# Decoder layer on one core: first modulation by slices of 256 features, squares of four units summed at once, second-norm modulation moved into the output projection

## The reference

```python
mod = silu(c) @ w_ada + b_ada                      # c: one row; w_ada: 1024 x 6144
shift1, scale1, gate1, shift2, scale2, gate2 = split(mod, 6)
h = rms_norm(x, norm1_g) * (1 + scale1) + shift1
q, k, v, qi, ki, wi, u_pool, g_attn, g_pool = split_cols(h @ w_in)
q, k = rms_norm per head of 64                     # 8 heads
attn = top-128 sparse attention(q, k, v, indexer qi, ki, wi)
y_attn = attn @ w_attn_br
y_pool = multiscale_pool(u_pool, w_grp, pool_scale) @ w_pool_br
merged = sigmoid(g_attn) * y_attn + sigmoid(g_pool) * y_pool
x = x + gate1 * (merged @ w_out)
h2 = rms_norm(x, norm2_g) * (1 + scale2) + shift2
x = x + gate2 * conv_ffn(h2, w_up, conv_w, conv_b, w_down)   # d_ff 2816, taps 3
```

## Time and profile before

| | |
|---|---|
| median of 3 runs (lowest to highest) | 754.72 us (754.32 to 757.94) |
| profiled execution: its own time, its span | 759.15 us, 757.2 us |
| PE busy | 739.7 us, 98% of the span |
| DVE, ACT, POOL busy | 379.0, 306.6, 312.3 us |
| DMA | 92.75 MB, mean 122 GB/s |
| mean granted clock of TensorE | 0.986 of 2.4 GHz |

### The profile page before, as it was taken

One profiled execution on the slowest core, in us unless ns is written; L12 is line 12 of the kernel. 1 busy time (PEld: TensorE's weight loads), 2 busy tenths in 40 slices (PEclk: granted clock), 3 DMA queues, 4 the chain that ended last, 5 costly groups with the idle time before them and its releaser, 6 DMA issues.

```text
span 757.2 us, 9497 instructions
## 1 busy us (share of the span) xinstructions
PE 739.7 (98%) x3568; PEld 597.2 (79%) x3568; DVE 379.0 (50%) x693; ACT 306.6 (40%) x501; POOL 312.3 (41%) x165
## 2 busy tenths in 40 slices
PE   4989999999999999999999999999999999999997
PEld 3467788888777777887899888888788888888886
DVE  2588699972446551774685435464443433004002
ACT  4224513256756763334455343434334343212120
POOL 1125338562623332547423444444444444443431
PEclk9969989999999999999999999999999999999999
DMA  8995511221113113644338344323323321233301
GB/s 327 381 338 204 187 55 57 71 97 56 57 57 112 57 56 107 262 159 128 97 95 267 112 111 112 91 76 112 101 68 110 111 99 68 84 112 112 137 2 56
DMA packets 83995, 92.75 MB, mean 122 GB/s; under 512 B 2035, under 2 KB 66287, under 8 KB 83951
## 3 DMA queue, kind: packets, MB, share of 16 engines
q1 hardware_dynamic: 82719, 87.43, 35.6%
q10 hardware_dynamic: 1232, 4.72, 1.7%
HBM read 90.05 MB, written 2.10 MB: 122 GB/s over the span
## 4 chain that ended last, share of the span: by engine, by line
PE 96%; DVE 1%; DMA 1%; ACT 1%; SPq 0%; issue 0%; DVEq 0%; ACTq 0%
PE bank L1471 42%; PE bank L1491 21%; PE bank L1480 21%; PE bank L1547 2%; PE bank L1741 1%; PE bank L1719 1%; PE bank L1707 1%; PE bank L1513 1%; PE bank L1625 1%; DMA xtok<-in_x_dram 1%; PE bank L1565 1%; PE bank L1614 1%; ACT junk L747 1%; PE bank L1518 1%; PE bank L1775 1%; PE bank L1532 0%
## 5 line engine op out<-in xcount | busy, mean ns | idle before, releaser
L650 POOL TENSOR_TENSOR wsplit<-stage,wsplit 128x1024 fp32r<-128x1024 f32 (+1 forms) x120 | 275.0, 2295 | 395.2 <-ACT wsplit L732 391.7
L1471 PE MATMUL bank<-hT,wsplit 128*128 128x512 f32 (+1 forms) x1264 | 295.3, 386 | 0.0
L1471 PEld LDWEIGHTS bank<-hT,wsplit 128*128 128x128 f32 x1264 | 231.8, 190 | 46.5 <-issue 0.9
L732 ACT ACTIVATE wsplit<-stage 128x1024 fp32r<-128x1024 f32 (+1 forms) x120 | 119.8, 1000 | 280.9 <-PE bank L1480 196.7
L1480 PE MATMUL bank<-hT,wsplit 128*128 128x512 f32 (+1 forms) x632 | 152.8, 384 | 0.0
L1480 PEld LDWEIGHTS bank<-hT,wsplit 128*128 128x128 f32 x632 | 114.7, 188 | 23.5 <-issue 0.8
L1491 PE MATMUL bank<-wsplit,guT 128*128 128x512 f32 x528 | 119.8, 389 | 0.0
L1491 PEld LDWEIGHTS bank<-wsplit,guT 128*128 128x128 f32 x528 | 99.1, 188 | 20.5
L1429 DVE SCALAR_TENSOR_TENSOR yb<-bank,conv,yb 128x511 f32<-128x511 f32 (+1 forms) x44 | 32.9, 749 | 65.1 <-ACT yb L1022 64.3
L1429 DVE SCALAR_TENSOR_TENSOR ya<-bank,conv,ya 128x511 f32<-128x511 f32 (+1 forms) x44 | 33.0, 749 | 59.2 <-ACT ya L1022 58.4
L1364 DVE TENSOR_TENSOR tmp_last<-bank,gate_row 128x512 f32<-128x512 f32 x8 | 5.5, 688 | 101.7 <-PE bank L1491 101.7
(11 more groups left out here) (188 smaller groups left out, 731.8 us busy)
## 6 DMA issues: line engine op xcount, KB each, us to landing
stage<-in_w_up_dram SPq DMA_DIRECT2D x44, 512.0 KB, 5.2
stage<-in_w_in_dram SPq DMA_DIRECT2D x17, 1024.0 KB, 5.3
stage<-in_w_down_dram SPq DMA_DIRECT2D x10, 1024.0 KB, 5.0
ada_early<-in_w_ada_dram SPq DMA_DIRECT2D x8, 1024.0 KB, 10.1
ada<-in_w_ada_dram SPq DMA_DIRECT2D x7, 1024.0 KB, 11.7
ada_mid<-in_w_ada_dram ACTq DMA_DIRECT2D x4, 1024.0 KB, 8.1
stage<-in_w_out_dram SPq DMA_DIRECT2D x4, 1024.0 KB, 6.1
ada_last<-in_w_ada_dram SPq DMA_DIRECT2D x4, 1024.0 KB, 11.1
```

Of the source, the lines that this page charges most:

```text
L650: pool.tensor_tensor(unit_split(n, 1), unit_source(n), unit_split(n, 0).bitcast(F32), ALU.subtract).then_inc(low, 1)
L732: me.did(act.activation(unit_split(n, 0), unit_source(n), ACT.Copy), high)
L1471: pe.matmul(out_bank[:, tokens], hi[:, k, :], rhs[:, part, k, tokens], start=k == 0 and part == 0, stop=False)
```

## The change

1. **Start.** x is normalised token tile by token tile before it is transposed (`xn`; the scaling by the root is on VectorE). shift1 and scale1 are made in four slices of 2 x 256 features: `load_first(q)` brings 128 x 8 x 512 values in two halves, in rows of 1 KB. `first_sums` multiplies them with `cpad` (silu(c), padded to 32 columns), four input blocks at once into four groups of 32 partitions of one bank, two rounds; ScalarE copies, `first_columns` sums over partitions into columns, and VectorE makes two blocks of `hT` from it. All seven first units (qi 0, 1, kw, q 0 to 3) are accumulated side by side in seven banks, input block by input block. Their weights come as items of 2 x 896 columns, one behind each slice, and their low parts are made on VectorE.
2. **Order.** v follows, with the index dots between its blocks, then u, then k. The four squares of q go to TensorE at once (`squares`: `halves`, padded to 32 columns, as weights, 512 tokens, four groups of partitions), are copied and transposed (`squares_turn`); the same for k.
3. **Second norm.** The row additions of shift2 and scale2 (j = 3, 4) are no longer made from `ada_early` beside q. ScalarE's queue loads them through the two `ada_mid` buffers in the output projection, VectorE adds the first set ahead of `gate_vector(0)` and the second behind it, both ahead of the residuals, and TensorE turns them into columns after the first and the second tile of the second half.
4. Window sums get a second pair of buffers; c is loaded from ScalarE's queue; two activation tables are called up early.

The core of the diff:

```diff
-ROW_TURN = {1: 0, 3: 1, 4: 2, 2: 3, 5: 4}
+ROW_TURN = {2: 0, 3: 1, 4: 2, 5: 3}
+FIRST = (("qi", 0), ("qi", 1), ("kw", 0), ("q", 0), ("q", 1), ("q", 2), ("q", 3))
...
+            def load_first(q):
+                for half in range(2):
+                    ks = slice(half * KQ, (half + 1) * KQ)
+                    for j in range(2):
+                        c0 = j * D + 2 * q * P
+                        sp.dma_start(ada_first[q][:, ks, 2 * j * P:2 * (j + 1) * P], ada[:, ks, c0:c0 + 2 * P]
+                                     ).then_inc(ada_in[q][half], 16)
...
             for n, item in enumerate(sch.items):
-                if n == NSTAGE:
-                    for q in range(KD // 2):
-                        load_early(3, q)
...
+                if n < KQ:
+                    load_first(n)
...
 # ScalarE
+            load_mid(4)
+            load_mid(5)
             high_parts(sch.unit["out", 1, NT - 1] + 1)
+            for n in range(6, 12):
+                load_mid(n)
...
 # VectorE
+            for t in range(NT):
+                dve.wait_ge(root_ok, t + 1)
+                me.did(dve.reciprocal(tstat[:, 3, t:t + 1], tstat[:, 2, t:t + 1]))
+                me.settle()
+                me.did(dve.tensor_scalar(xn[:, t, :], xtok[:, t, :], tstat[:, 3, t:t + 1], None, ALU.mult), xn_ok)
...
+            for q in range(KQ):
+                first_vectors(q)
+                for k in (2 * q, 2 * q + 1):
...
+                    me.did(dve.tensor_scalar(full1[:, k % 2, :], xT[:, k, :], gs[:, 0, k:k + 1], mod[:, k:k + 1],
+                                             ALU.mult, ALU.add), n_ok)
+                for k in (2 * q, 2 * q + 1):
+                    first_low(k)
+                    low_parts(k + 1)
...
             merged_low(KD - 1)
+            for q in range(KD // 2):
+                mod_rows(3, q)
             gate_vector(0)
+            for q in range(KD // 2):
+                mod_rows(4, q)
...
 # TensorE
+            def first_sums(q):
...
+                for half in range(2):
+                    pe.wait_ge(ada_in[q][half], 32)
+                    for g in range(KQ):
+                        k = half * KQ + g
+                        mm = pe.matmul(OB[32 * g:32 * (g + 1), :], cpad[:, k, :], ada_first[q][:, k, :],
+                                       start=half == 0, stop=half == 1)
+                mm.then_inc(sums_ok, 1)
...
+            for k in range(KD - 1):
+                first_products(k, h_hi, 0, 0, start=k == 0)
+                if k % 2:
+                    first_columns(k // 2 + 1)
+                first_products(k, h_lo, 1, 0)
+                first_products(k, h_hi, 0, 1).then_inc(used, 1)
+                if k % 2 == 0 and k < KD - 2:
+                    first_sums(k // 2 + 1)
...
+            def squares(part):
+                pe.wait_ge(sq_ok, KA * (part + 1))
...
+                for g in range(KA):
+                    mm = pe.matmul(SUMS[part][0][32 * g:32 * (g + 1), :], halves[:, :], sq[part][g][:, :],
+                                   start=True, stop=True)
+                mm.then_inc(sq_used, 1)
...
+            index_dots(0)
+            await_bank(pe, ("v", 0))
+            value_high(0, 0, 3)
+            index_dots(2)
+            value_high(0, 3, 6)
+            index_dots(4)
...
                 if t == 1:
                     await_drained(pe, ("wo", 0, NT - 1))
                     pe.wait_ge(gate_ok, 2)
+                    pe.wait_ge(mod_ok, 2)
...
+                if t == 0:
+                    pe.wait_ge(gate_ok, 2)
+                    mod_columns(3)
                 if t == 1:
+                    mod_columns(4)
                     x2_turn(0)
```

More of the change, by code:

```diff
@@ L138, in split, with first @@
             self.unit[name] = len(self.units) - 1
+    def first(self):
+        for q in range(KQ):
+            self.items.append(("first", "in", (C_Q, C_QI), 2 * q, 2 * q + 2, 1))
+            self.last_use.append(None)
+            for r in range(2):
+                self.units.append((1, r, KS))
+                self.house()
+                self.item_of.append(q)
+                self.last_use[q] = ("unit", len(self.units))
+        for at, name in enumerate(FIRST):
+            self.opens(name, "dve", FIRST_BANK[at])
+        self.ring = NBANK - 1
     def block_rows(self, w, k0, k1, half, home=None):
@@ L179, in schedule @@
     s = Schedule()
[L180 removed]
+    s.first()
+    for kind, n in (("v", KA), ("u", KA)):
         for m in range(n):
@@ L1464, in _, with high_products @@
         def _(pe):
-            def high_products(n, out_bank, rhs, tokens=slice(0, S)):
+            def high_products(n, out_bank, rhs, tokens=slice(0, S), blocks=None):
                 hi = unit_split(n, 0)
                 pe.wait_ge(high, n + 1)
-                for k in range(sch.units[n][0]):
+                for k in blocks or range(sch.units[n][0]):
                     for part in range(2):
@@ L1472, in high_products, with low_products @@
                                   start=k == 0 and part == 0, stop=False)
-            def low_products(n, out_bank, rhs, tokens=slice(0, S), signal=used):
+            def low_products(n, out_bank, rhs, tokens=slice(0, S), signal=used, blocks=None):
                 nk = sch.units[n][0]
@@ new lines, in first_columns, with first_products @@
+            def first_columns(q):
+                pe.wait_ge(row_ok, q + 1)
+                for n in range(4):
+                    mm = pe.matmul(OB[:, MC + n:MC + n + 1], rowsum[:, n * P:(n + 1) * P], ones[:, 0:1],
+                                   start=True, stop=True)
+                mm.then_inc(col_ok, 1)
+            def first_products(k, made, part, a, names=FIRST, start=False, stop=False):
+                pe.wait_ge(made, k + 1)
+                pe.wait_ge((high, low)[a], k + 1)
+                for name in names:
+                    at = FIRST_AT[FIRST.index(name)]
+                    mm = pe.matmul(bank(name)[:, :], unit_split(k, a)[:, 0, at:at + P], hT[:, part, k, :],
+                                   start=start, stop=stop)
+                return mm
```

585 lines of the change are left out of this document (288 added, 297 removed).

## The result

The changed kernel takes 782.59 us (median of 4 runs, 781.21 to 785.16); the kernel before, run beside it, 755.05. The ratio is 1.0366 with a 95% interval of 1.0334 to 1.0398: 3.7% slower, where the prediction said 748.8 and 0.8% faster. The profiled execution has a span of 779.4 us against 757.2 before, and the prediction's sum was 751.3. So 28.1 us of span have to be found.

A forecast was written before the change was run, and what follows sets the result against it. TensorE, carrying 96% of the span, was taken as the bound. 70.7 + 648.0 + 8.8 + 23.8 = 751.3 us of span against 757.2, or 748.8 from the median, 0.8% faster; range 739 to 762.

The forecast's parts named there:

- Part 1: Start: first product at 22.3, TensorE then the limit, all seven first units done at 70.7 us, bounds 68 and 79.
- the rival of the column groups: Start and squares: column groups don't run four at once; two at once gives 761.4, none 781; chance 0.07.
- Part 2: From the first units to the attention: 658.8 us to come, 648.0 after removals, 8.8 added back.
- the same state (q done, without the index dots): End of the first units: the old kernel reaches this point at 98.43, leaving 658.8 of 757.2 us.
- the waits of 1.2 us: Behind the first units: index dots wait on ScalarE, whose queue now also has the queries' squares and copies; 1.2 us.
- The rival of unseen waits: First stage or attention's start: waits of 3 to 7 us not seen, giving 754, no difference; chance 0.20.
- Part 3: Output projection: row additions delay the x2 turn by 21.3 us, plus 2.5 for the lower clock, 23.8 in sum.
- two or three: Output projection: row additions meeting GpSimd's low parts, up to 3.36 us instead of 1.28; last row at 387, upper bound 389.6.
- 2.5 of lower clock: Output projection: TensorE returns at the lower clock after two long stretches standing still; 2.5 us, between 1.7 and 3.4.
- The rival of the two slow buffers: Output projection: loads through two buffers take longer, 8.1 us each giving 756.9, 10.5 giving 764.1; chance 0.18.
- the 648.0: Everything after the first units: 648.0 us left once squares turns, column turns and a lower-clock loss are removed.
- 740: Output projection: rival that row additions are covered better, loads landing back to back, ending at 378; chance 0.10.

The follow-up runs named there:

- e2: The changed kernel with `halves` moved behind all other tiles, so hT and the rest lie at the addresses of the kernel before: 772.09 us, ratio 1.0194.
- e9: e2 with six of the eight loads for the shift and gain rows cut to 128 of 1024 columns, all additions kept: 763.49 us, one run.
- e13: e2 with loads cut as in e9 and the shift and gain rows' additions after the first product cut to 128 columns: 754.85 us, one run.
- e14: e2 with the four subtractions for `own` on VectorE ahead of the shift rows, instead of on GpSimd: 767.51 us, ratio 1.0166.
- e5: e2 with one line moved, VectorE's mixed(1) ahead of two top-k rounds instead of behind them: 764.71 us, ratio 1.0109.
- e6: e2 with the output projection reordered, all work kept: two loads earlier, gate and residuals before the gain rows finish, gain columns later: 761.43 us, ratio 1.0069.
- e16: The kernel before with a gap of 256 bytes ahead of hT: 757.13 us, one run beside a median of 756.17.
- e11: The kernel before with a gap of 512 bytes ahead of hT: 757.82 us, one run beside 758.43.
- e3: The kernel before with a gap of 32 bytes ahead of hT: 769.98 us, ratio 1.0173.
- e1: The kernel before with a gap of 96 bytes ahead of hT: 771.68 us, ratio 1.019.
- e4: The kernel before with a gap of 128 bytes ahead of hT: 767.42 us, ratio 1.0139.
- e10: The kernel before with 96 bytes ahead of all its tiles, distances between them kept: 756.59 us, one run beside 758.43.
- e12: e2 with the first two loads of the shift rows issued two merged blocks earlier: 763.86 us, one run.

## Why the prediction was wrong

**Part 1 was right in mechanism, and nearly in size.** Units done at 70.29 for 70.7, the sums of a slice 1.85 for 2.0. Four column groups do run at once, so the rival of the column groups is refuted, and the squares took 1.06 for 1.1 as well. Two errors cancel in the 0.4 us: the first product came 1.7 us earlier than forecast, since the first sums began 1.3 us sooner and took 2.3 us for 3.4, not being at the lower clock; and the units took 1.3 us longer from there (49.7 for 48.4), the slower products among the causes.

**Part 2 failed at its first number.** The prediction equated "the same state (q done, without the index dots)" with 98.43 in the trace of before. The products that run up to that point include the whole unit u0; q3 had ended at 91.03. TensorE in order of time, kernel before:

```profile
91.03 0.96 PE L1614 MATMUL bank<-kiT,qiT 64*128 64x512 f32 x6
...
92.84 3.94 PE L1471 MATMUL bank<-hT,wsplit 128*128 128x512 f32 x16
96.62 1.98 PE L1480 MATMUL bank<-hT,wsplit 128*128 128x512 f32 x8
```

From 98.43 to the first scores the kernel before runs thirteen units, the changed kernel fourteen from 70.29 on. So one unit of 5.44 us was counted as done in the changed kernel and was not. This is a slip in reading the order of time, and nothing on the chip. It alone moves 751.3 to 756.7, from "faster" to "no difference".

**Part 2, the waits of 1.2 us.** The rival of unseen waits, 3 to 7 us, came true in one place: k3, 2.30 us of idling and 1.65 us for the lower clock behind it (146.84 to 152.22 is 5.38, where k2 took 3.73; granted clock 0.63, then 0.75). The prediction looked for a late VectorE only at the mean of q and k. There VectorE was not late at all; in order of time, changed kernel:

```profile
146.05 0.74 DVE L1287 SCALAR_TENSOR_TENSOR mix<-bank,vec,mix 128x512 fp32r<-128x512 f32 x1
...
159.65 0.19 DVE L1338 TENSOR_SCALAR stat<-bank 128x32 f32<-128x32 f32 x1 [6.55 <-PE bank L1683]
```

It idles 6.55 us, more than the 2 forecast. The cover was thin earlier, at `mixed(1)`. A queue that is in time at its end can be late in its middle. Of the remaining 2.9 us of the stage's 12.3, the slower products take 1.6: without k3's wait and clock the stage is 95.2 us here and 93.7 in e2. The last 1.3 were not taken apart. The waits of the index dots are not it, 0.79 and 0.20 for the 1.2 forecast.

**Part 3, 23.8 us: nearly right, for reasons that the runs bear out.** Counted from the start of the projection, the last row was forecast after 45.3 us (341.75 to 387) and came after 49.5 (326.27 to 375.75). The term that was mis-sized is the meetings with GpSimd: "two or three", taken at 2.7 us, and there were four, 2.14 + 9.95 us where 0.75 + 3.9 was undisturbed, 7.4 us. The end of the turn came 62.1 us after the start, for 56.9 and 2.5 of lower clock. The rival of the two slow buffers did not come true. The three reloads of the odd buffer on which it rests took 7.3, 5.2 and 5.2 us from the last addition on it to the next (350.29 to 357.56 and so on), 1.5 us more than 3 x 5.4, and it needed 5.9. e9 prices the loads at 7 us all the same, and e13 and e14 show that neither they nor the additions are the pace alone. That the stage is off by only 3.5 us is in part luck: the first load landed 0.9 us sooner than forecast, and behind the turn TensorE took 12.7 us to the up projection for 11.9 before, so most of the 2.5 us for the clock was not lost there.

**What no step of the prediction had: the place of the tiles.** It carried the up and down projections over unchanged, as part of the 648.0. They took 10.4 us more, and the attention's stage 2.3 more; in e2 the two stages take 368.1 and 154.5, as forecast. The full diff shows the cause in plain sight, `halves` growing from [P, 2] to [P, 32] ahead of `hT`, yet no row of before could have told what it costs.

**The rivals' figures.** The prediction calls them spans, but 756.9, 764.1, 754 and 740 are worked out from the median, 748.8, and only 761.4 and 781 from the span, 751.3. With the spans of each the two slow buffers would have been at 759.4 and 766.6.

So, of 28.1 us: 10.4, 2.3 and 1.6 for the tiles' place, 5.4 for the slip, 4 for k3, 3.5 in the output projection, and 1.3 not taken apart, less the 0.4 gained at the start. e2, e5 and e6 each take one of the three causes on the chip away; e2 gives back less than its 14.3 us, as its waits grow by 4. What stays open is why a distance off a multiple of 256 bytes costs TensorE 3%, and why the same wait is followed by the lower clock in one execution and not in another.

## What to carry to other kernels

When a tile in front of others changes its size, keep the later tiles where they were, or compare the spacing of untouched matmuls before anything is explained: a unit of the last stage, which the change doesn't reach, tells it in two rows. When a sum starts from "the same state" in a trace, list the products that had run by then. And work moved beside another engine's work on the critical path is not priced by its own duration: here loads and additions slowed by GpSimd hid each other, and only taking both away at once (17.3 us against 6.0 and 7.0) showed it.

## What the runs showed of the hardware

- TensorE, 512 columns of fp32r against 128x128 weights: 5.44 us for 24 matmuls if the distance between the two tiles read is 0, 256 or 512 bytes off that of the kernel before, itself a multiple of 256 (e16, e11); 5.58 to 5.60 at 32, 96 and 128 (e3, e1, e4). The same shift of 96 bytes for both tiles costs nothing (e10).
- A wait of TensorE of 2.99 us was followed by sixteen matmuls in 6.60 us in e2 (granted clock 0.50 at first) and in 5.37 us in e12, where the full clock takes 3.63 (e5). A wait of 1.96 us was followed by a granted clock of 0.50 in e2 and of 1.00 in e12.
- Four column groups with one 512-column f32 product each took 1.06 us together (changed kernel), where one alone is two records of 0.43.
- An addition with two SBUF inputs of 1024 columns on VectorE took 1.28 us, and 3.32 us beside GpSimd's subtractions; these took 2.97 us each instead of 2.41 (changed kernel).
